# Two transformer blocks on one core: a group norm's averages in rounded high and low parts, memory keys in 256-column chunks, and an activation's low parts taken ahead of a weight's

## The reference, cut to what matters

```python
def conformer_conv(z, w_dw, b_dw, gn_g, gn_b):        # z: (B, 256, 512)
    a, g = jnp.split(z, 2, axis=-1)
    y = a * jax.nn.sigmoid(g)
    y = depthwise_conv(y, w_dw) + b_dw                # 31 taps, causal
    y = y.reshape(Bn, S, C_GROUPS, HEAD_DIM)          # 4 groups of 64 channels
    y = layer_norm(y, gn_g.reshape(...), gn_b.reshape(...))   # mean and variance per group
    return jax.nn.silu(y.reshape(Bn, S, C_WIDTH))

def memory_cross_attention(h, m, w_q, w_kv, w_o):
    k, v = jnp.split(m @ w_kv, 2, axis=-1)            # each (256, 1024): 4 heads of 256
    ...
```

## Time and profile before

| | |
|---|---|
| median of three executions | 747.65 us |
| the profiled execution, its own time | 747.14 us |
| its span in the profile | 745.4 us |
| PE busy | 737.5 us (99%), 4024 matmuls |
| DVE busy | 532.4 us (71%) |
| ACT busy | 408.0 us (55%) |
| POOL busy | 39.3 us (5%) |
| granted TensorE clock | 0.999 of full speed on average |

### The profile page before, as it was taken

How to read it: one execution, slowest core, us unless ns; L and a number is a source line. 1 busy time by engine, 2 the same in 40 slices (tenths; PEclk the granted TensorE clock), 3 DMA queues, 4 the chain that set the end, 5 groups by cost and what they waited for, 6 DMA issues and landing times. The chain is left out here.

```text
span 745.4 us, 9905 instructions
## 1 busy us (share of the span) xinstructions
PE 737.5 (99%) x4024; PEld 634.3 (85%) x4024; DVE 532.4 (71%) x628; ACT 408.0 (55%) x519; POOL 39.3 (5%) x69
## 2 busy tenths in 40 slices
PE   9999999999999999999999999999999999999996
PEld 9988888889988888888888897788987888888885
DVE  6888946885766666666789999786758655566564
ACT  6678378544545545444763585674647443454442
POOL 0200002120000000000200000020003000000000
PEclk9999999999999999999999999999999999999999
DMA  9966365554565456666466536364165566555531
GB/s 340 287 229 223 128 242 209 170 172 168 174 222 170 170 173 204 210 203 213 157 198 205 191 113 226 116 234 148 44 215 169 159 218 226 174 207 181 165 120 57
DMA packets 81373, 138.39 MB, mean 186 GB/s; under 512 B 3884, under 2 KB 42672, under 8 KB 81200
## 3 DMA queue, kind: packets, MB, share of 16 engines
q1 hardware_dynamic: 79472, 132.69, 53.2%
q10 hardware_dynamic: 1856, 5.06, 1.9%
HBM read 136.69 MB, written 1.05 MB: 185 GB/s over the span
## 5 line engine op out<-in xcount | busy, mean ns | idle before, releaser
L1334 DVE TENSOR_TENSOR low<-raw,high 128x2048 fp32r<-128x2048 f32 (+1 forms) x120 | 271.3, 2278 | 101.9 <-ACT high L702 96.3
L702 ACT ACTIVATE high<-raw 128x2048 fp32r<-128x2048 f32 (+3 forms) x134 | 234.6, 1769 | 108.2 <-PE wide L2120 84.5
L2120 PE MATMUL wide<-act_hl,high 128*128 128x512 f32 (+1 forms) x960 | 239.0, 364 | 0.3 <-DVE act_hl L1399 0.2
L2120 PEld LDWEIGHTS wide<-act_hl,high 128*128 128x128 f32 x960 | 171.0, 190 | 28.6 <-issue 0.5
L2120 PE MATMUL wide<-high,act_hl 128*128 128x512 f32 x528 | 170.1, 394 | 0.5 <-DVE act_hl L1431 0.3
L2120 PE MATMUL wide<-act_hl,low 128*128 128x256 f32 x832 | 160.1, 282 | 0.0
L2120 PEld LDWEIGHTS wide<-act_hl,low 128*128 128x128 f32 x832 | 127.6, 191 | 2.7 <-DVE low L1382 0.2
L2120 PEld LDWEIGHTS wide<-high,act_hl 128*128 128x128 f32 x528 | 99.1, 188 | 23.4 <-issue 1.5
L2120 PE MATMUL wide<-low,act_hl 128*128 128x512 f32 x264 | 102.9, 390 | 0.0
L702 ACT ACTIVATE arena<-wide 128x512 f32<-128x512 f32 x62 | 35.1, 596 | 94.5 <-PE wide L2120 94.3
L2120 PE MATMUL bank<-high,hid_hl 128*128 128x512 f32 x256 | 80.1, 389 | 0.0
(11 more groups left out here) (219 smaller groups left out, 698.6 us busy)
## 6 DMA issues: line engine op xcount, KB each, us to landing
raw<-in_w_ff_dram SPq DMA_DIRECT2D x32, 1024.0 KB, 5.4
raw<-in_w_in_dram SPq DMA_DIRECT2D x27, 1024.0 KB, 5.3
raw<-in_w_ffn_in_dram SPq DMA_DIRECT2D x40, 512.0 KB, 4.9
raw<-in_w_ffn_out_dram SPq DMA_DIRECT2D x11, 1024.0 KB, 6.9
raw<-in_w_xkv_dram SPq DMA_DIRECT2D x8, 1024.0 KB, 5.0
raw<-in_w_o_dram SPq DMA_DIRECT2D x4, 1024.0 KB, 5.0
raw<-in_w_out_dram SPq DMA_DIRECT2D x4, 1024.0 KB, 5.3
raw<-in_w_xq_dram SPq DMA_DIRECT2D x4, 1024.0 KB, 5.2
```

Source lines behind the costliest of these rows:

```text
L702: return act.activation(dst, src, func, **k)
L1334: tt(part(low, g), part(raw, g), f32(part(high, g)), SUB).then_inc(sem.low_by_dve, 1)
L2120: return pe.matmul(dst, lhs, rhs, start=start, stop=stop, skip_group_check=loose)
```

## The change

Four edits, all in the second block but for a constant:

1. `block_mean` becomes a rounded matrix (F32R), made on GpSimd (POOL) by three multiplications in place of three memsets. `group_mean` and `group_var` each become two F32R matmuls, of a high and a low part. ACT writes the high part (`conv_high`, `square_high`), DVE the low part (`conv_low`, `square_low`), 128x512 each. `group_mean` moves from row tile 4 to row tile 6 of `("kv",2)`, `group_var` behind its neighbouring transposes.
2. `("kv",1)` is split into `("kv",1,0)` and `("kv",1,1)`, in way H, with the twelve transposes between them. ACT and DVE each get two instructions for it (`low_part`, `half_total`); ACT's two copies of the C way go. PE's wait on `half_sum` for the first half stands ahead of `moba_values(0)`, that for the second ahead of `mix_top(0)`.
3. On DVE, the low parts of the turned tokens (`norm_split(2)`) and a `half_total` come ahead of a weight's low part, and one more `half_total` ahead of the next weight's.
4. On ACT, one weight's high part comes ahead of the tanh in `zc_tanh`.

```diff
-    for c in range(1, 3):
-        add_kv(c)
+    for i in range(2):
+        add(("kv", 1, i), w["w_xkv_2"], 0, KD, [(0, NB + i * 256, 256)], 256)
+    add_kv(2)
...
+            def conv_high():
+                act.wait_ge(sem.conv_done, 2)
+                f(glu_r, flat(cv), ACT.Copy).then_inc(sem.gn_high, 1)
+            def square_high():
+                act.wait_ge(sem.gn_sq, 1)
+                f(glu_r, cs, ACT.Copy).then_inc(sem.gn_high, 1)
...
+            split_high(chunks[("zc", 1)][0][0] + LEAD + 1)
             zc_tanh()
...
-            ahead_of_half(("kv", 1), 0)
+            ahead_of(("kv", 1, 0), "H")
+            act.wait_ge(sem.x_low, 2)
+            low_part(k_mem[:, 0:2, :])
             moba_turned(0)
-            ahead_of_half(("kv", 1), 1)
-            kv_in(1)
+            ahead_of(("kv", 1, 1), "H")
+            low_part(k_mem[:, 2:4, :])
             moba_scale(1)
             high_of_bank(1, bank[4], sem.mo_o)
-            ahead_of(("kv", 2), "T")
+            ahead_of_half(("kv", 2), 0)
+            conv_high()
+            ahead_of_half(("kv", 2), 1)
             kv_in(2)
             high_of_bank(0, bank[7], sem.ya2_turned)
+            square_high()
             group_sd()
...
+            def conv_low():
+                dve.wait_ge(sem.gn_high, 1)
+                tt(cs_r, flat(cv), f32(glu_r), SUB).then_inc(sem.conv_done, 1)
+            def square_low():
+                dve.wait_ge(sem.gn_high, 2)
+                tt(cv_r, cs, f32(glu_r), SUB).then_inc(sem.gn_sq, 1)
...
             scale_x()
-            ahead_of(("kv", 0, 0), "H")
+            me.used += 1
+            me.pairs += 1
             half_total(k_mem[:, 0:2, :])
             norm_split(2)
-            ahead_of(("kv", 0, 1), "H")
+            split_low(chunks[("kv", 0, 0)][0][0] + LEAD + 1)
+            me.used += 1
+            me.pairs += 1
             half_total(k_mem[:, 2:4, :])
+            split_low(chunks[("kv", 0, 1)][0][0] + LEAD + 1)
...
-            ahead_of_half(("kv", 1), 0)
+            ahead_of(("kv", 1, 0), "H")
+            half_total(k_mem[:, 0:2, :])
             conv_dw(28, DW_TAPS)
             conv_bias()
-            ahead_of_half(("kv", 1), 1)
-            ahead_of(("kv", 2), "T")
+            ahead_of(("kv", 1, 1), "H")
+            half_total(k_mem[:, 2:4, :])
+            ahead_of_half(("kv", 2), 0)
+            conv_low()
+            ahead_of_half(("kv", 2), 1)
             low_of_bank(1, b=bank[4])
             spatial()
             group_mean()
             low_of_bank(0, b=bank[7])
+            square_low()
             kv_low(2, me.pair())
...
             def var_and_turn():
-                pe.wait_ge(sem.gn_sq, me.seen("gn_sq"))
+                pe.wait_ge(sem.gn_sq, 1)
+                moba_turn(1, (0, 1))
+                pe.wait_ge(sem.gn_sq, 2)
                 group_var()
-                moba_turn(1, (0, 1))
...
             def group_mean():
-                pe.wait_ge(sem.conv_done, me.seen("conv_done", 2))
-                mm(bank[6][:, :], block_mean[:, :], flat(cv)).then_inc(sem.gn_mean, 1)
+                pe.wait_ge(sem.conv_done, 3)
+                mm(bank[6][:, :], block_mean[:, :], glu_r, True, False)
+                mm(bank[6][:, :], block_mean[:, :], cs_r, False, True).then_inc(sem.gn_mean, 1)
...
-            products(("kv", 1), "C", is_mem=True, at={4: turn_first})
+            products(("kv", 1, 0), "H", is_mem=True)
+            turn_first()
             pe.wait_ge(sem.v2_in, 2)
+            products(("kv", 1, 1), "H", is_mem=True)
+            pe.wait_ge(sem.half_sum, me.seen("half_sum"))
             pe.wait_ge(sem.mo_t, me.seen("mo_t", 4))
             moba_values(0, bank[4])
             spatial()
-            products(("kv", 2), "T", is_mem=True, at={4: group_mean})
+            products(("kv", 2), "T", is_mem=True, at={6: group_mean})
             pe.wait_ge(sem.act_hl, me.seen("act_hl"))
-            pe.wait_ge(sem.kv_in, 4)
+            pe.wait_ge(sem.half_sum, me.seen("half_sum"))
```

More of the change, by code:

```diff
@@ L143, in __init__ @@
         self.bias_and_gate_w = new("bias_and_gate_w")
+        self.gn_high = new("gn_high")
         self.gn_mean = new("gn_mean")
@@ L302, in two_blocks @@
         ident = sb("ident", [P, P])
-        block_mean = sb("block_mean", [P, P])
+        block_mean = sb("block_mean", [P, P], F32R)
         if_bias = sb("if_bias", [4, 2])
@@ L412, in two_blocks @@
         dist = carve(DIAG)
+        glu_r = arena_r[:, top[0]:top[0] + 2 * T]
         glu = carve(2, T + DW_TAPS - 1)
+        cv_r = arena_r[:, top[0]:top[0] + 2 * T]
         cv = carve(2, T)
         cx = carve(2 * T)
+        cs_r = arena_r[:, top[0]:top[0] + 2 * T]
         cs = carve(2 * T)
@@ L602, in constants @@
                 pool.wait_ge(sem.pool_step, me.step())
-                pool.tensor_scalar(neg_one_r, neg_one, 1.0, None, ALU.mult).then_inc(sem.consts, 1)
[L604 to L608, removed]
+                pool.tensor_scalar(block_mean[:, :], neg_one, 0.0, None, ALU.mult).then_inc(sem.pool_step, 1)
+                pool.wait_ge(sem.pool_step, me.step())
+                for a in (0, 64):
+                    pool.tensor_scalar(block_mean[a:a + 64, a:a + 64], neg_one[a:a + 64, a:a + 64], -1 / 64, None,
+                                       ALU.mult).then_inc(sem.consts, 1)
+                pool.wait_ge(sem.consts, me.seen("consts", 3))
+                pool.tensor_scalar(neg_one_r, neg_one, 1.0, None, ALU.mult).then_inc(sem.consts, 1)
                 pool.wait_ge(sem.consts, me.seen("consts"))
@@ L1012, in kv_in @@
             def kv_in(c):
[L1013 to L1017, removed]
+                copy_pair(v_high[c - 2][:, 0, :], v_high[c - 2][:, 1, :], sem.kv_in)
             def xq_high(i):
@@ L1246, in _ @@
             copy_pair(v2[:, 0, :], v2[:, 1, :], sem.v2_in)
-            ahead_of_half(("kv", 1), 0)
+            ahead_of(("kv", 1, 0), "H")
+            act.wait_ge(sem.x_low, 2)
+            low_part(k_mem[:, 0:2, :])
             moba_turned(0)
-            ahead_of_half(("kv", 1), 1)
-            kv_in(1)
+            ahead_of(("kv", 1, 1), "H")
+            low_part(k_mem[:, 2:4, :])
+            me.seen("half_sum", 2)
             moba_scale(1)
             high_of_bank(1, bank[4], sem.mo_o)
-            ahead_of(("kv", 2), "T")
+            ahead_of_half(("kv", 2), 0)
+            conv_high()
+            ahead_of_half(("kv", 2), 1)
             kv_in(2)
             high_of_bank(0, bank[7], sem.ya2_turned)
+            square_high()
             group_sd()
@@ L1850, in kv_low @@
                 for i, b in enumerate(pair):
-                    dve.wait_ge(sem.kv_in, 2 * c + i + 1)
+                    dve.wait_ge(sem.kv_in, 2 * c + i - 1)
                     tt(v_low[c - 2][:, i, :], b[:, :], f32(v_high[c - 2][:, i, :]), SUB).then_inc(sem.x_low, 1)
@@ L2531, in group_mean @@
             def group_mean():
-                pe.wait_ge(sem.conv_done, me.seen("conv_done", 2))
-                mm(bank[6][:, :], block_mean[:, :], flat(cv)).then_inc(sem.gn_mean, 1)
+                pe.wait_ge(sem.conv_done, 3)
+                mm(bank[6][:, :], block_mean[:, :], glu_r, True, False)
+                mm(bank[6][:, :], block_mean[:, :], cs_r, False, True).then_inc(sem.gn_mean, 1)
             def group_var():
-                mm(bank[4][:, :], block_mean[:, :], cs).then_inc(sem.gn_var, 1)
+                mm(bank[4][:, :], block_mean[:, :], glu_r, True, False)
+                mm(bank[4][:, :], block_mean[:, :], cv_r, False, True).then_inc(sem.gn_var, 1)
             def x_scores(i):
```

## The result

| | before | changed |
|---|---|---|
| median | 747.40 us (747.18 to 748.11, 5 executions) | 754.43 us (754.01 to 755.84, 5) |
| ratio, with its 95% interval | | 1.0097 [1.0082, 1.0111] |
| profiled execution, own time | 747.14 us | 754.01 us |
| its span | 745.4 us | 752.3 us |

What follows compares the result with a forecast made beforehand. PE was taken to bound the kernel (busy 737.5 of 745.4 us), apart from waits for DVE. 4.25 - 0.3 - 0.2 + 1.7 - 0.65 + 0.6 = +5.4 us, stated as 752.8 us with half the median's offset; range 750.4 to 756.0.

Steps and rivals of the forecast that it cites:

- gate 1: At the norm, PE's `zc` 0 waits for the weight's low part, which DVE now writes later: +4.25 us.
- clock stays up in `zc` 0: The forecast's assumption that PE runs `zc` 0 at the upper clock level after the stall; forecast's chance 0.55.
- wait at `k2`: PE's 0.4 us wait for DVE where `k2` starts was to go, taken as -0.3 us.
- gate 2: Ahead of the attention's values, PE must now wait for DVE's `half_total` (`half_sum`): a stall of 1.7 us.
- `group_norm`'s reciprocal: DVE's reciprocal at the group norm was to come at 472.9 instead of 467.47, a shift of +5.4 us.
- gate 3: At `mix_bottom(0)` PE waits for `low_of_bank(2)`, ending a rigid 13.04 us DVE and ACT chain; passes on +5.4 us.
- The gain of 0.54 us on the mean: Two F32R matmuls (0.455 us) replace the mean's fp32 product (0.995 us) on PE: -0.54 us.
- the parts of the square: ACT's `square_high` and DVE's `square_low`, needed before the variance, come late ahead of the group norm: +0.6 us.
- The clock falls in the stall: Rival: PE's idleness before `zc` 0 lowers the clock, eight pairs at half pace add 2.8 us: 755.6 us; chance 0.23.
- the forecast's own case: Whole kernel with the clock staying up: 752.8 us, likeliest between 751.6 and 754.0; chance 0.55.
- the term (0.455): At the averages, the F32R pair for one average was taken to cost PE two normal steps, 0.455 us.
- the sign named for it: In the trace, `block_mean` matmuls at the averages were to show 0.39 us each instead of 0.592.

Runs made afterwards that it cites:

- e9: The changed kernel run once more with no edit: 755.16 us, ratio 1.0102 to the kernel before.
- e1: The kernel before with edit 3 alone (DVE writes the tokens' low parts ahead of the weight's): 753.60 us, ratio 1.0077.
- e2: The changed kernel with edit 3 undone (DVE's order at the norm as before): 748.92 us, ratio 1.0017.
- e4: The changed kernel with PE's wait for `half_sum` moved behind the attention's values and the spatial gate: 753.38 us, ratio 1.0074.
- e5: The changed kernel with edit 3 undone and PE's wait for `half_sum` moved behind the values and the spatial gate: 747.04 us, ratio 0.9997.
- e3: The changed kernel with 18 matmuls, their result overwritten, filling PE's stall ahead of `zc` 0: 753.22 us, ratio 1.0073.
- e10: The changed kernel with nine filler matmuls, their result overwritten, in PE's stall ahead of `zc` 0: 753.67 us, ratio 1.0083.
- e6: The kernel before with edit 1 alone (the averages as products of rounded parts): 747.83 us, ratio 1.0004.
- e7: As e5, but only the mean goes by rounded parts and the variance stays an fp32 product: 746.81 us, ratio 0.9991.
- e8: As e7, with `low_of_bank(2)` ahead of the low part of `mix_top` 1's weight on DVE: 746.66 us, ratio 0.9988.

## Why the prediction came out as it did

The steps, as the prediction put them, against the trace of the changed kernel:

| step | predicted | measured |
|---|---|---|
| gate 1: `zc` 0 starts | 380.6, +4.25 | 380.55, +4.21 |
| clock stays up in `zc` 0 (0.55 and more), falls (0.23, +2.8) | stays | falls; +1.5, in e9 +2.7 |
| wait at `k2` | gone | gone |
| gate 2: the stall | 1.7 | 1.63 |
| the values start | +5.45 | +6.91 (455.11) |
| `group_norm`'s reciprocal | 472.9, +5.4 | 474.32, +6.85 |
| end | +5.4 | +6.88 |

**What held.** Gate 1 is the order of DVE's two instructions and nothing else: e1 makes it, e2 unmakes it. Gate 2 is the place of the wait: the stall was mis-sized by 0.07 us, and e4 and e5 take it away (it is 1.6 in e2 too, where the clock stays up, and 1.3 in the profiles of e3 and e10, at the slower pace of the pairs). The end hangs on the group norm's reciprocal (gate 3), which eleven profiles show to within 0.07 us. The gain of 0.54 us on the mean, undone by the parts of the square, is seen in e6 as no change, and in the difference of e5 and e7: with the square's parts gone the reciprocal comes 467.18 - 466.76 = 0.42 us sooner (the sum had put these parts at 0.6). The three starts below gate 1 are all off by the same 1.4 to 1.5 us, so one step failed, ahead of all of them.

**The step that failed** is the choice between the forecast and its first rival, *The clock falls in the stall*. The forecast let `zc` 0 run at the upper level. The clock fell in every profile in which PE idled for 4.4 us there (the changed kernel twice, e1, e4), and in none of those where the stall was filled, half filled or absent. The rule of the Trainium skill (TensorE: Matmul & The Clock Gate, "Why this matters for your kernels") that was put beside this rival agrees with these traces, and the forecast should have followed it. The prediction's argument against it was that the trace shows only one fall, at the end; but that row was one observation for the fall after 3.8 us of idleness and there was none against it, and a gap of 4.5 us is longer. A chance of 0.23 was not what the rows supported. The stated range holds the result only because it was drawn up to the middle of this rival; the forecast's own case ended at 754.0.

The rival's price was too high, and wrong as a fixed size. It was put at 2.8 us, eight pairs that each take 0.353 us longer. A pair at the lower level takes 0.64 us, 0.29 more, so eight cost 2.3. The traces show five pairs and 1.5 us (changed), seven pairs, not all of them at the lower level throughout, with 1.6 (e1: 385.00 - 380.93 less 7 x 0.353) and 2.0 (e4: 385.31 - 380.80), and nine with 2.7 (e9). In the profiled execution of the changed kernel it is 1.5 us, which with the +5.4 of the sum gives the +6.9 measured.

The profiles in which `zc` 0 starts as late and the clock holds let that be tested. From the first transpose ahead of the norm to the reciprocal it is 467.47 - 372.78 = 94.69 us before, 474.32 - 372.80 = 101.52 in the changed kernel, 473.78 - 373.50 = 100.28 in e3 and 473.21 - 372.92 = 100.29 in e10. So without the fall the shift is +5.6, with it +6.8. e3 and e10 have the slower pace of the pairs; the estimate for the 32 pairs of `zc`, on which DVE's chain hangs, is 32 x 0.0065 = 0.2 us, which would make it the forecast's +5.4. The sum thus holds where its assumption on the clock does.

That the median lies between the two cases, and in the stated range with room to spare, is partly luck: three of the first five executions were in the group of the higher mean clock. In e9 three of four were in the other, and their times are the rival's. The rival's 755.6 lies among the five slower executions (755.06 to 755.84), the forecast's 752.8 0.4 us below the kernel whose stall was filled (753.22). Over all nine executions the median is 755.06.

**Smaller misses.** The averages' pairs last 0.62 us together (465.76) where 0.39 each was said to be seen; two starts 0.23 apart and one end give just that, so the term (0.455) stands and the sign named for it was clumsy. By the medians e5, which was to gain 0.5 to 0.8, gained 0.46, and e7, which was to gain 0.9 to 1.2, gained 0.7. Counted from the transposes ahead of the norm, the reciprocal comes 0.47 us sooner than before in e5 (467.18 - 372.96 = 94.22) and 0.93 in e7 (466.76 - 373.00 = 93.76), close to or in the expected ranges; all three profiles have the faster pace. Medians of eleven executions don't settle what is left.

**What the version without the gates is worth.** e8, with the rounded mean, the fp32 variance, both gates gone and gate 3 loosened, has the lowest median of all kernels here: 746.66 us, 0.12% under the kernel before (0.03% to 0.21%). Its interval lies just under no change, but the gain is less than the 0.2% that was taken as the least that can be told.

## What to carry to other kernels

Before work is moved ahead of other work on an engine, look at what the next engine needs for its first instruction: all its operands, not the one that is being hurried. Here the order had the activation's first low parts 0.3 us sooner (375.02 in place of 375.32) and the weight's 4.4 us too late. A gap on TensorE can be dearer than its length: behind the one of 4.4 us the matmuls ran at nearly half pace for 3 to 6 us. If such a gap can't be avoided, matmuls that compute nothing can be cheaper than idleness (e3). And where everything hangs on one instruction (here the reciprocal, with 271.8 us behind it in eleven profiles), positions in the traces are a finer ruler for small edits than medians, if both ends of the distance are chosen so that nothing else lies between; here that ruler has a spread of 0.13 us.

## What the runs showed of the hardware that was not expected

The time at the 1.2 GHz level after the same stall of 4.4 us differs from run to run of one program: measured from the start of `zc` 0 it was 3.4 us in the changed kernel's profile, 6.1 in e9's. The moment of the fall differs too, and with it what is left of the lower level when the matmuls start. By the windows view the granted clock was at 0.50 from 380.6 to 384.0 in the changed kernel (the fall came with the first matmul behind the stall), from 381.5 to 384.9 in e1 (half a microsecond after it), from 378.4 to 385.2 in e4 and from 379.8 to 386.7 in e9. The stall of 1.6 us at the values never showed a lower clock in a profile, nor did 2.3 us in that of e10, yet e4's clock was down after 2.0 us of its stall. And pairs of matmuls of one shape kept one of two paces, 0.347 or 0.353 us, over a stretch of 20 us at a granted clock of 1.00, even in profiles whose instructions up to there were the same (e7 and e8); no run shows why.
